# Fewer slots for the mix stage in the row-by-row plan of a hybrid decoder step

## The reference

```
h   = RMSNorm(x) * (1 + scale1) + shift1              (shift, scale, gate from silu(c))
z   = h @ W_in                                        queries, keys, values, gates, conv input
x  += gate1 * ([RMSNorm(NSA attention) ; conv branch] @ W_out)
h2  = RMSNorm(x) * (1 + scale2) + shift2
PEER: q = h2 @ peer_q; scores against 2 x 128 sub keys per head, top 16 of their sums,
      for each of 8 heads x 16 experts e:  y += softmax weight * gelu(h2 . u[e]) * v[e]
x  += gate2 * y
```

## Time and profile before

| | |
|---|---|
| median of 3 executions | 1948.86 us |
| lowest, highest | 1946.51, 1961.23 us |
| the profiled execution | 1946.51 us |
| its span, first to last instruction | 1944.6 us |
| mean granted TensorE clock | 0.856 |

### The profile page before, as it was taken

One profiled execution on the slowest core, in us unless ns is written; L12 is line 12 of the kernel. 1 busy time (PEld: TensorE's weight loads), 2 busy tenths in 40 slices (PEclk: granted clock), 3 DMA queues, 4 the chain that ended last, 5 costly groups with the idle time before them and its releaser, 6 DMA issues.

```text
span 1944.6 us, 27857 instructions
## 1 busy us (share of the span) xinstructions
PE 1490.2 (77%) x9567; PEld 832.6 (43%) x9567; DVE 1258.6 (65%) x3411; ACT 763.5 (39%) x2179; POOL 783.3 (40%) x676
## 2 busy tenths in 40 slices
PE   7868777969689988869668879689789785866535
PEld 4747643436345533446214447345455242423101
DVE  1565777945878788845986655984565645443755
ACT  1431345742355567642246642232222323232322
POOL 0000234423234354522443334776565767422532
PEclk9989887888789998978868989889899777786858
DMA  9986999989999999999999999999999999999997
GB/s 395 335 318 233 420 408 419 421 337 415 415 387 405 410 420 403 375 421 420 419 421 398 420 420 419 390 390 401 360 379 387 360 398 348 402 410 392 382 414 301
DMA packets 133447, 756.73 MB, mean 389 GB/s; under 512 B 17182, under 2 KB 36542, under 8 KB 47282
## 3 DMA queue, kind: packets, MB, share of 16 engines
q0 software_dynamic: 82432, 578.86, 73.7%
q1 hardware_dynamic: 50875, 176.10, 23.4%
HBM read 750.19 MB, written 9.29 MB: 391 GB/s over the span
## 4 chain that ended last, share of the span: by engine, by line
PE 29%; DVE 19%; DMA 18%; issue 7%; ACT 6%; POOL 5%; another core or an unknown queue 1%; SPq 0%; ACTq 0%; DVEq 0%
PE bank L1463 11%; DMA expert_rows<-in_expert_uv,expert_index 10%; DVE expert_rows L2768 8%; PE bank L1206 3%; POOL weight_units L2816 3%; PE bank L860 3%; PE bank L1334 3%; POOL expert_rows L2812 2%; PE bank L1190 2%; PE bank L797 2%; DMA weight_units<-in_w_out_units 2%; DMA weight_units<-in_peer_q_units 1%; DMA gate_or_shift_and_scale<-mod_dram 1%; DVE gate_or_shift_and_scale L2226 1%
## 5 line engine op out<-in xcount | busy, mean ns | idle before, releaser
L2812 POOL DMA_INDIRECT expert_rows<-in_expert_uv,expert_index x544 | 641.4, 1179 | 1095.2 <-PE bank L1463 747.7
L2768 DVE CUSTOM_DVE_ANT_0 expert_rows<-expert_rows,h_rows 128x1024 f32<-128x1024 f32 x544 | 660.6, 1222 | 300.3 <-DMA expert_rows<-in_expert_uv,expert_index 280.9
L1463 PE MATMUL bank<-expert_rows,weight_diagonals 64*64 64x512 f32 x4096 | 605.0, 708 | 143.0 <-ACT weight_diagonals L2048 130.0
L2028 ACT ACTIVATE group_gelu<-group_dots 128x2 f32<-128x2 f32 x272 | 55.8, 205 | 757.8 <-DVE group_dots L2768 677.2
L1463 PEld LDWEIGHTS bank<-expert_rows,weight_diagonals 64*64 64x64 f32 x4096 | 153.9, 151 | 430.5 <-issue 237.9
L2048 ACT ACTIVATE weight_diagonals<-consts_sb,group_weights 128x64 f32<-128x64 f32 (+1 forms) x544 | 159.0, 340 | 16.7 <-ACT group_weights L2038 0.7
L1206 PE MATMUL bank<-stage_room,weight_units 128*128 128x128 f32 x1024 | 129.2, 286 | 13.9 <-ACT stage_room L1867 7.4
L1206 PEld LDWEIGHTS bank<-stage_room,weight_units 128*128 128x128 f32 x1024 | 122.7, 199 | 34.9 <-issue 22.1
L2038 ACT ACTIVATE group_weights<-group_gelu,expert_gate 128x1 f32<-128x1 f32 x544 | 131.6, 289 | 9.4
L2028 ACT ACT_TABLE_LOAD x74 | 94.9, 1283 | 1.3
L2226 DVE SCALAR_TENSOR_TENSOR conv_out<-stage_room,small_weights,conv_out 128x128 f32<-128x128 f32 (+1 forms) x360 | 94.9, 310 | 0.1
(11 more groups left out here) (392 smaller groups left out, 1983.1 us busy)
## 6 DMA issues: line engine op xcount, KB each, us to landing
weight_units<-in_peer_q_units SPq DMA_DIRECT2D x40, 1024.0 KB
weight_units<-in_w_in_units SPq DMA_DIRECT2D x23, 1024.0 KB
weight_units<-in_w_out_units SPq DMA_DIRECT2D x19, 1024.0 KB
weight_units<-in_w_ada_units SPq DMA_DIRECT2D x13, 1024.0 KB
expert_rows<-in_expert_uv,expert_index POOLq DMA_INDIRECT x544
weight_units<-in_w_units SPq DMA_DIRECT2D x8, 1024.0 KB
expert_rows<-in_w_ada_units SPq DMA_DIRECT2D x7, 1024.0 KB, 11.0
gate_or_shift_and_scale<-mod_dram SPq DMA_DIRECT2D x11, 512.0 KB
```

Of the source, the lines that this page charges most:

```text
L1463: last = mm(e.bank[2 * a + c][o * HD:(o + 1) * HD, :], e.diag[ps, m % (NG * GR)], e.ring[ps, m % RING, cs], start=first, stop=final)
L2028: do(e.act_v[:, p], e.dots[:, p], ACT.Gelu_apprx_tanh).then_inc(e.s_gelu, 1)
L2768: vec.tensor_tensor_reduce(out=row, in0=row, in1=e.h2[:, i % 2], scale=1.0, scalar=0.0, op0=ALU.mult, op1=ALU.add, accum_out=e.dots[:, q % ...
L2812: pool.indirect_dma_start(e.ring[:, n % RING], None, e.io["expert_uv"], bass.IndirectOffsetOnAxis(ap=e.eidx[:, i % 2, j:j + 1], axis=0)).t ...
```

## The change

The stage mix of tiles 1 to 4 is given 18 slots and a length of 10, in place of 23 slots and a length of 12.5. Tile 0 has its own entry (`FIRST_SLOTS`), which is (18, 10) already. No operation, wait or transfer is added or removed in the stage itself.

```diff
 SLOTS_OF = {"ada1": (10, 10), "ada2": (14, 40), "ada3": (6, 3), "x": (4, 3), "glu": (18, 13), "z": (16, 10),
-            "conv": (43, 0), "cmp": (11, 5.5), "mix": (23, 12.5), "query0": (20, 11), "query1": (19, 12.5), "topk0": (31, 8),
+            "conv": (43, 0), "cmp": (11, 5.5), "mix": (18, 10), "query0": (20, 11), "query1": (19, 12.5), "topk0": (31, 8),
             "topk1": (31, 22), "sc": (42, 21), "satt": (90, 60)}
```

## The result

The changed kernel took 1963.32 us (median; 1952.23 to 1967.38), the kernel before, run beside it, 1948.01 us (1941.48 to 1961.88). The ratio is 1.0057, 95% interval [1.0036, 1.0079]: the change makes the kernel slower, by about 0.6% or 11 us. (The medians are of 14 executions of each kernel; the ratio takes in 34 of the changed one, whose median is 1958.7 us.) Weighted by their intervals the three give 1.0041, give or take 0.0015, or 8 us. That interval is too narrow: 1.0057 and 1.0011 lie further apart than their own intervals allow for, so the sessions differ by more than the scatter within them. Ratios leave out executions that took over 1.5% longer than the fastest of the same kernel beside them, one of 3366 us with tile 4 alone among them.

The account below looks back on a forecast made before the run. DMA engines bound the kernel: bytes over rate plus idle holes. From the profiled 1946.51 us, -4 + 2 + 0 + 0 gave 1944.5, or 1946.9 in medians; forecast 1946 us, range 1935 to 1960.

Parts of the forecast that it names:

- The reading of the kernel: Whole run: time is bytes over rate plus DMA idle holes; 756.73 MB, 400 GB/s from 206 to 1930 us.
- The plan: Stage placement: pace goes from 0.990 to 1.010 rows a unit; other stages stay within two rows of their places.
- Mix 1, -4: Tile 1's mix: its two handshakes come apart, closing between 0 and 8 us of DMA hole; taken as -4 us.
- Mix 3, +2: Tile 3's mix: both handshakes now precede one pair, opening a hole of 0 to 8 us; taken as +2 us.
- the hole moves: Rival, chance 0.14: tile 3's mix costs the full 8 us, tile 1's gives back only 2; 1955 us.
- Query0's wait, 0: PE's wait for `h2` after each of four mixes: priced 0 to 8.4 us each, taken as 0.
- query0's wait drains the ring: Rival, chance 0.11: PE stands 10 us before a pair, four times; 1982 us for all four, 1957 for one.
- The sign that was named for it: Sign of a wrong forecast: a window of DMA share under 0.8 in the 10 us before any turning of `h2`.
- PE stands for nearly the full 10 us: At query0's first slot: the wait for `h2` follows mix directly, so PE waits nearly all 10 us.
- Six or more rows in flight are 15 us: At query0's wait: gathered rows under way cover 15 us, the reason given for taking 0.
- all under gathers: After PE's waits: one more slow pair in each of four mixes, some 5 us of PE's time, hidden by gathers.
- The rest, 0: Holes elsewhere, from rows and page gathers that shift by one: bounds -5 and +5 us, taken as 0.

Follow-up runs that it names:

- tile 4 alone: Only the samples' mix (tile 4) set to 18 slots and length 10, the rest as in the kernel before; ratio 1.0005 [0.9984, 1.0027].
- tile 3 alone: Only tile 3's mix set to 18 slots and length 10, the rest as in the kernel before; ratio 1.0038 [1.0014, 1.0062].

## Why the prediction was wrong

*The reading of the kernel* held. Bytes and rate stayed, and the time went with the holes.

*The plan* held: 1.010, the groups of slots before each pair, and mix 1's order. The timeline of mix 1 in the changed kernel, to be read against the earlier trace rows:

```profile
398.65 3.69 PE L1463 MATMUL bank<-expert_rows,weight_diagonals 64*64 64x512 f32 x16
...
404.08 1.09 PE L1181 MATMUL bank<-consts_sb,stage_room 128*128 128x128 f32 x8 [1.74 <-DVE stage_room L2488]
...
405.11 1.95 PE L1463 MATMUL bank<-expert_rows,weight_diagonals 64*64 64x512 f32 x16
...
407.36 0.94 POOL L2812 DMA_INDIRECT expert_rows<-in_expert_uv,expert_index  x1 [1.39 <-PE bank L1463]
...
409.44 0.69 DVE L2493 TENSOR_TENSOR stage_room<-stage_room,small_weights 128x512 f32<-128x512 f32 x1 [4.27 <-ACT stage_room L1854]
...
416.88 1.95 PE L1463 MATMUL bank<-expert_rows,weight_diagonals 64*64 64x512 f32 x16
...
419.13 0.94 POOL L2812 DMA_INDIRECT expert_rows<-in_expert_uv,expert_index  x1 [9.59 <-PE bank L1463]
```

The turning was forecast at 405.3 and came at 404.08; pair 56's gather at 410, came at 407.36; pair 58's at 421, came at 419.13.

*Mix 1, -4:* its handshakes' idle time went from 8.4 to 5.3, 2.5 and 5.4 us, a mean of -4.0. Right, and also in that the hole split in two.

*Mix 3, +2:* 0.0 before, 1.9, 0.6 and 1.5 after, a mean of +1.3. Right for the changed kernel. That the full 8 us is real, as the rival "the hole moves" had it, is shown by the kernel with tile 3 alone (8.7 us there) and tile 4 alone (5.5 in mix 3).

*Query0's wait, 0:* this step failed. The idle time of the DMA engines behind the wait measured +12.3, +9.6 and +9.7 us over the three profiles, a mean of +10.5. With -4.0 and +1.3 the sum is +7.8 us (mix 2's and mix 4's handshakes stay within 0.1), against 8 us measured. That the two agree so closely is partly luck, since the three ratios lie 0.46% apart. The prediction had the mechanism, as the rival with chance 0.11, "query0's wait drains the ring", but priced it at all of 8.4 us or nothing for a mix. It came at 2.6 us a mix on average, from almost nothing to 4.5, with tiles 1 and 3 in all three profiles. The sign that was named for it, a DMA share under 0.8 in the 10 us before the turning of `h2`, would not have shown it: from 431.6 to 441.6 us the share was 1.02, and the hole came behind the turning. Three things in its working were wrong:
- The plan was counted pair by pair for the handshakes, but not for this wait. Counted so, PE's slots before pair 64 in tile 1 and pair 200 in tile 2 now hold it, where it stood before pairs 66 and 202; in tiles 3 and 4 it stays before pairs 298 and 476, but mix's last filled slots now come right before it.
- "PE stands for nearly the full 10 us" counted the wait alone. What the DMA engines see is the gap between gathers. To the wait's end it adds the turning and the pair itself, 1.97 + 3.69 us, which in the changed kernel stand behind the wait. From the end of PE's pair at 433.3 to the end of the next at 447.2 are 14 us.
- "Six or more rows in flight are 15 us" took rows that DVE hadn't used for rows that hadn't landed. At the last gather (435.78) there were seven rows that DVE had not taken, 67 to 73, but the DMA engines drained about 10 us later, four rows' worth. The cover of shares of 1.00 and 1.01 was read off a kernel in which the next pair still ran before the wait ended; that cover was what the empty slots gave.

*The clock.* The pair behind the wait took 3.69 us at 443.53, the next of its kind 1.95 at 450.92. I had put this slow pair "all under gathers". It stands between the wait and the next gather, so its 1.7 us lengthen the gap and so the hole. The granted clock was 0.53 from 443.5 to 447.3, next to the lower of its two levels, after 8.3 us in which PE stood, and 1.00 from 447.3. The rule of the Trainium skill that was named there (TensorE: Matmul & The Clock Gate, HAM oscillation) agrees with the row. In the kernel before the pair of these rows was slow as well (3.39 us at 437.66), but ahead of the wait, where it delayed nothing that the DMA engines were short of.

*The rest, 0:* elsewhere nothing of the change was found; holes come and go by a few us from one profile to the next.

## What to carry to other kernels

Empty slots and spare length around a stage can be what lets the bottleneck's orders go out before a wait; before you remove them, ask which orders will stand behind it. Price such a wait from the last order before it to the first after it, everything that the engine runs in between included, and set against it what is still to land, not what is still to be used. Where it is too long, hold the waiting work back by one unit of the other rather than fill the time: here two rows of lead less took the holes away, and together with fewer slots in the same length gave the quickest kernel. Hold it in the unchanged kernel too, as here: part of the gain may have nothing to do with the change.

## What the runs showed that was not expected

- Small stores that were issued while the DMA engines were full (share 1.02 from 737.7 to 761.3) took 23.6 us to release the engine that waited for them (the last issued at 737.71, released at 761.30). DVE stood for 11.48 us of that.
- The same kernel, unchanged, measured 1.0057, 1.0041 and 1.0011 against the kernel before in three sessions, with intervals of 0.002 to 0.003 either way. Differences of 0.3% need more than one session.
- A plan changed in one tile moved which slots share a pair in the tiles before and behind it, through the pace. The kernel with tile 3 alone had more idle time at the handshakes (16.9 us, of which 8.2 are mix 1's old hole and 8.7 new in mix 3) than the one with all four tiles changed (3.2 to 7.3), so the tiles' effects don't add up.
